# Sums of weight blocks made by adding transfers on GpSimd's queue, and the seven products of a pair in another order

## The reference

```
def _squared_relu_mlp(h, w1, w2):
    return jnp.square(jax.nn.relu(h @ w1)) @ w2

for layer in range(DEPTH_2):
    ...
    x = x + _rms_norm(mix, norm_mix_post[layer])
    hn = _rms_norm(x, norm_ffn_pre[layer])
    x = x + _rms_norm(_squared_relu_mlp(hn, mlp_w1[layer], mlp_w2[layer]), norm_ffn_post[layer])
```

## Time and profile before

| | us |
|---|---|
| median of 3 runs | 1752.04 (1751.86 to 1753.19) |
| the profiled execution | 1751.83 |
| its span | 1750.1 |
| TensorE busy in the span | 1720.5 |
| VectorE busy | 1058.1 |
| ScalarE busy | 869.3 |
| GpSimd busy | 367.2 |

### The profile page before, as it was taken

One profiled execution on the slowest core, in us unless ns is written; L12 is line 12 of the kernel. 1 busy time (PEld: TensorE's weight loads), 2 busy tenths in 40 slices (PEclk: granted clock), 3 DMA queues, 4 the chain that ended last, 5 costly groups with the idle time before them and its releaser, 6 DMA issues.

```text
span 1750.1 us, 21182 instructions
## 1 busy us (share of the span) xinstructions
PE 1720.5 (98%) x8319; PEld 1376.0 (79%) x8319; DVE 1058.1 (60%) x1408; ACT 869.3 (50%) x1410; POOL 367.2 (21%) x197
## 2 busy tenths in 40 slices
PE   7999999999999999999999999999999999999998
PEld 5888777778787767876988888888876798888886
DVE  6611567685976367954467576745457247686855
ACT  4324566557635353254563535336677356354542
POOL 0443322123244233433400000004410330000000
PEclk9999999999999999999999999999999999999999
DMA  8524322221132322311232231322320241414031
GB/s 314 209 92 120 97 61 60 74 73 55 67 121 80 109 73 72 108 49 57 91 131 100 93 128 65 121 73 64 96 66 1 97 145 48 147 47 169 25 130 75
DMA packets 83935, 166.25 MB, mean 95 GB/s; under 512 B 6041, under 2 KB 8222, under 8 KB 83838
## 3 DMA queue, kind: packets, MB, share of 16 engines
q1 hardware_dynamic: 83838, 164.93, 28.3%
HBM read 157.64 MB, written 2.10 MB: 91 GB/s over the span
## 4 chain that ended last, share of the span: by engine, by line
PE 92%; DVE 4%; ACT 2%; issue 1%; POOL 1%; DMA 0%; SPq 0%; DVEq 0%; ACTq 0%; POOLq 0%
PE PDT L779 10%; PE PDT L781 10%; PE PDT L780 10%; PE PDT L768 9%; PE PDT L770 8%; PE PDT L769 8%; PE PM L970 4%; PE PM L965 4%; PE PM L963 4%; PE PM L1153 2%; PE PM L1427 2%; PE PDT L1388 2%; PE PM L1388 2%; PE PM L1120 1%; PE PM L1180 1%
## 5 line engine op out<-in xcount | busy, mean ns | idle before, releaser
L2201 POOL TENSOR_TENSOR wlo<-wraw,whi 128x512 fp32r<-128x512 f32 (+5 forms) x112 | 324.2, 2911 | 933.6 <-ACT whi L1589 758.8
L779 PE MATMUL PDT<-hhi,whi 128*128 128x512 f32 x796 | 312.3, 392 | 0.5 <-POOL wlo L2201 0.5
L781 PE MATMUL PDT<-hhi,wlo 128*128 128x512 f32 x796 | 310.2, 390 | 0.0
L780 PE MATMUL PDT<-hlo,whi 128*128 128x512 f32 x796 | 310.1, 390 | 0.0
L1705 ACT ACTIVATE whi<-wraw 128x2048 fp32r<-128x2048 f32 x78 | 149.5, 1917 | 276.1 <-PE PM L970 120.5
L2876 DVE TENSOR_TENSOR wlo<-wraw,whi 128x2048 fp32r<-128x2048 f32 x78 | 178.7, 2291 | 160.9 <-ACT whi L1705 160.7
L768 PE MATMUL PDT<-whi,hhi 128*128 128x512 f32 (+1 forms) x592 | 233.4, 394 | 1.1 <-DVE hlo L2611 0.6
L770 PE MATMUL PDT<-whi,hlo 128*128 128x512 f32 (+1 forms) x592 | 227.9, 385 | 0.0
L769 PE MATMUL PDT<-wlo,hhi 128*128 128x512 f32 (+1 forms) x592 | 227.8, 385 | 0.0
L1589 ACT ACTIVATE whi<-wraw 128x2048 fp32r<-128x2048 f32 (+3 forms) x71 | 129.3, 1821 | 173.7 <-PE PDT L770 75.8
L779 PEld LDWEIGHTS PDT<-hhi,whi 128*128 128x128 f32 x796 | 149.5, 188 | 31.5 <-issue 1.5
(11 more groups left out here) (409 smaller groups left out, 2873.5 us busy)
## 6 DMA issues: line engine op xcount, KB each, us to landing
wraw<-in_mlp_w SPq DMA_DIRECT2D x64, 1024.0 KB, 5.1
wraw<-in_w_in SPq DMA_DIRECT2D x26, 1024.0 KB, 5.1
wraw<-in_even_w_in SPq DMA_DIRECT2D x16, 1024.0 KB, 5.2
w_ada<-in_w_ada SPq DMA_DIRECT2D x11, 1024.0 KB, 12.9
wraw<-in_w_out SPq DMA_DIRECT2D x8, 1024.0 KB, 4.9
swapped<-qk_sb SPq DMA_DIRECT2D x16, 256.0 KB, 7.2
wraw<-in_even_w_out SPq DMA_DIRECT2D x4, 1024.0 KB, 4.9
wraw<-in_odd_w_o SPq DMA_DIRECT2D x4, 1024.0 KB, 4.9
```

The lines of the kernel that those rows point to most:

```text
L779: mm(bank, sth, hi[:, k0 + k, :], start=start and k == 0, stop=False)
L780: mm(bank, sth, lo[:, k0 + k, :], start=False, stop=False)
L781: last = mm(bank, stl, hi[:, k0 + k, :], start=False, stop=stop and k == 3)
L2201: part = g.tensor_tensor(wlo[base % 2][:, cols], wraw[base % 2][:, cols], fl(whi[base % 2][:, cols]), ALU.subtract)
```

## The change

Four things change, all in the two MLPs except for the last.

1. The sums of blocks of `w2` are no longer made by VectorE. GpSimd issues transfers from HBM that add what they bring onto what stands in the slot (`accum_op=ALU.add`), five per pair, and each waits for the one before it (semaphore `w_added`). Slot e gets B11 by a plain load, then two transfers make it the operand of P6, and a fifth, after P6's split, that of P4. Slot b gets B12 and one transfer, for P7. P1's slot gets one transfer after P1's split, for P5. ScalarE's `raw_hi` waits on `w_added` for these four (`ADDED`, `SUMMED`).
2. The seven products come in the order P1, P2, P6, P5, P7, P3, P4 (before: P1, P5, P6, P2, P7, P3, P4), and VectorE's low parts and additions follow it.
3. SyncE loads five plain blocks per pair instead of four, B11 twice and B22 and B21 for P3 and P2, in another order and into slots by another rule (`pair_loads`).
4. The space for descriptors of software transfers is 2048 bytes instead of 1024, the arena of buffers starts at a multiple of 64 bytes instead of 512, and the small tile `scratch1` lies in the arena.

The core of the diff:

```diff
@@ -67,11 +67,20 @@
 MLP_UNITS = 41
 CHUNKS = [0, 2, 4, 13, 15, 24, 26, 35]
 PAIRED = [6, 17, 28]
-ROLES = [(2, 3, 0, 1), (1, 3, 0, 2), (2, 3, 0, 1)]
-MLP_LOADS = [(0, 0), (1, 1), (2, 2), (3, 3), (4, 0), (5, 1),
-             (6, 2), ("b", 6, 3), (11, 0), (9, 1), (13, 1), (14, 3), (15, 0), (16, 2),
-             (17, 1), ("b", 17, 3), (22, 0), (20, 2), (24, 2), (25, 3), (26, 0), (27, 1),
-             (28, 2), ("b", 28, 3), (33, 0), (31, 1), (35, 1), (36, 3), (37, 0), (38, 2), (39, 3), (40, 2)]
+P1, P2, P6, P5, P7, P3, P4 = range(7)
+
+
+def pair_loads(d, a, e, b, plain):
+
+    return [((d, "e"), e), ((d, P1), a), ((d, P2), plain), ((d, "b"), b), ((d, P3), plain)]
+
+
+MLP_LOADS = [((0, 0), 0), ((1, 0), 1), ((2, 0), 2), ((3, 0), 3), ((4, 0), 0), ((5, 0), 1)]
+MLP_LOADS += pair_loads(6, 3, 2, 1, 0) + [((13, 0), 3), ((14, 0), 1), ((15, 0), 0), ((16, 0), 2)]
+MLP_LOADS += pair_loads(17, 1, 3, 2, 0) + [((24, 0), 1), ((25, 0), 2), ((26, 0), 0), ((27, 0), 3)]
+MLP_LOADS += pair_loads(28, 2, 1, 3, 0) + [((35, 0), 2), ((36, 0), 3), ((37, 0), 0), ((38, 0), 1), ((39, 0), 2),
+                                           ((40, 0), 3)]
+SUMMED = {P6: ("e", 2), P7: ("b", 3), P5: (P1, 4), P4: ("e", 5)}
 
 
 def phase_table():
@@ -113,9 +122,13 @@
 
     for name, (u0, _, _, units) in PH.items():
         if name in ("mlp0", "mlp1"):
-            for *key, slot in MLP_LOADS:
+            for (d, part), slot in MLP_LOADS:
                 slot = (u0 + slot) % 2 if slot < 2 else slot
-                load(u0 + key[0] if len(key) == 1 else (u0 + key[1], "b"), slot)
+                load((u0 + d, part) if isinstance(part, str) else u0 + d + part, slot)
+            for p, d in enumerate(PAIRED):
+                for n, (part, done) in SUMMED.items():
+                    of = table[u0 + d, part] if isinstance(part, str) else table[u0 + d + part]
+                    table[u0 + d + n] = (of[0], 16 * (15 * (name == "mlp1") + 5 * p + done))
         else:
             for u in range(u0, u0 + units):
...
-    A0 = (cursor[0] + 511) // 512 * 512
+    A0 = (cursor[0] + 63) // 64 * 64
...
             for p, d in enumerate(PAIRED):
                 c = 2 * p
                 split(CHUNKS[c + 1])
+                down((u0 + d, "e"), c, 0)
+                split(CHUNKS[c + 1] + 1)
                 down(u0 + d + P1, c, 0)
-                split(CHUNKS[c + 1] + 1)
+                split(CHUNKS[c + 2])
+                down(u0 + d + P2, c + 1, 0)
+                split(CHUNKS[c + 2] + 1)
                 down((u0 + d, "b"), c, 1)
-                split(CHUNKS[c + 2])
+                split(d + P2)
                 down(u0 + d + P3, c + 1, 1)
-                split(CHUNKS[c + 2] + 1)
-                down(u0 + d + P2, c + 1, 0)
+                split(d + P5)
+                up(c + 3, 0)
                 split(d + P7)
-                up(c + 3, 0)
                 up(c + 3, 1)
                 split(d + P3)
                 if p < 2:
...
                 product(P1, 0, True, base)
-                product(P5, 1, True, 0)
+                product(P2, 1, True, 0)
                 product(P6, 0, False, base + 1)
-                product(P2, 1, True, base + 3)
-                product(P7, 0, False, base + 4)
+                product(P5, 1, True, base + 2)
+                product(P7, 0, False, base + 3)
                 product(P3, 1, True, base + 5)
                 product(P4, 0, False, base + 6)
...
-            def raw_hi(o, slot=None, summed=0):
+            def raw_hi(o):
 
                 u = u0 + o
-                if summed:
-                    act.wait_ge(S("w_summed"), 12 * layer + summed)
-                elif u in RAW:
-                    slot, loaded = RAW[u]
-                    act.wait_ge(S(f"w_loaded{slot}"), loaded)
+                slot, loaded = RAW[u]
+                act.wait_ge(S("w_added" if (u0, o) in ADDED else f"w_loaded{slot}"), loaded)
                 act.wait_ge(S("w_used"), u - 1)
...
+
+            def added(key, c, h, count, after=None):
+
+                slot, loaded = RAW[key]
+                if count > 1:
+                    pool.wait_ge(S("w_added"), 16 * (count - 1))
+                pool.wait_ge(S(f"w_loaded{slot}"), loaded)
+                if after is not None:
+                    pool.wait_ge(S("w_split"), u0 + after + 1)
+                g.dma_start(wview(wraw[slot], 4, 512), w2_v[layer][:, 4 * c:4 * c + 4, 512 * h:512 * h + 512],
+                            accum_op=ALU.add).then_inc(S("w_added"), 16)
+
+            for p, d in enumerate(PAIRED):
+                c, n = 2 * p, 15 * layer + 5 * p
+                added((u0 + d, "e"), c, 1, n + 1)
+                added((u0 + d, "e"), c + 1, 1, n + 2)
+                added((u0 + d, "b"), c + 1, 1, n + 3)
+                added(u0 + d + P1, c, 1, n + 4, d + P1)
+                added((u0 + d, "e"), c + 1, 0, n + 5, d + P6)
...
-            def add_raw(to, other, loaded):
-
-                slot, value = RAW[loaded]
-                dve.wait_ge(S(f"w_loaded{slot}"), value)
-                v.tensor_tensor(wraw[to][:, :], wraw[to][:, :], wraw[other][:, :], ALU.add).then_inc(S("w_summed"), 1)
...
             def products(p):
 
-                a, b, c, d = [(u0 + slot) % 2 if slot < 2 else slot for slot in ROLES[p]]
                 o = PAIRED[p]
-                add_raw(a, c, u0 + o + P3)
-                gather(p, P1, 0, 0, 0, ALU.add, -3)
-                add_raw(b, c, u0 + o + P3)
-                raw_lo(o + P6, a)
+                gather(p, P1, 0, 0, 0, ALU.add, -6)
+                raw_lo(o + P6)
+                gather(p, P2, 1, 0, 0, ALU.add, 1)
+                raw_lo(o + P5)
+                gather(p, P6, 0, 0, 1, ALU.subtract, -1)
+                raw_lo(o + P7)
                 gather(p, P5, 1, 1, 1, ALU.subtract, -2)
-                gather(p, P5, 1, 0, 1, ALU.subtract, -1)
-                raw_lo(o + P2)
-                add_raw(a, d, u0 + o + P2)
-                gather(p, P6, 0, 0, 1, ALU.subtract, 3)
-                raw_lo(o + P7, b)
-                gather(p, P2, 1, 0, 0, ALU.add, 1)
+                gather(p, P5, 1, 0, 1, ALU.subtract, 3)
                 raw_lo(o + P3)
-                gather(p, P7, 0, 1, 1, ALU.subtract, 2)
-                raw_lo(o + P4, a)
-                gather(p, P3, 1, 0, 1, ALU.subtract, 4)
+                gather(p, P7, 0, 1, 1, ALU.subtract, 4)
+                raw_lo(o + P4)
+                gather(p, P3, 1, 0, 1, ALU.subtract, 5)
                 raw_lo(o + 7)
                 gather(p, P4, 0, 1, 0, ALU.add, 0)
...
-                a, b = [(u0 + slot) % 2 if slot < 2 else slot for slot in ROLES[p][0:2]]
-                add_raw(a, b, (u0 + PAIRED[p], "b"))
-                raw_lo(PAIRED[p] + P5, a)
+                raw_lo(PAIRED[p] + P2)
                 products(p)
...
-    nc = bacc.Bacc("TRN2", target_bir_lowering=False, num_devices=1, dynamic_dma_scratch_size=1024)
+    nc = bacc.Bacc("TRN2", target_bir_lowering=False, num_devices=1, dynamic_dma_scratch_size=2048)
```

32 lines of the change are left out of this document (10 added, 22 removed).

## The result

| | before | after |
|---|---|---|
| median (20 runs each) | 1752.03 us | 1755.11 us |
| lowest to highest | 1751.81 to 1755.07 | 1753.69 to 1758.00 |
| the profiled execution | 1751.83 | 1754.89 |
| its span | 1750.1 | 1752.7 |

The ratio is 1.0017, with a 95% interval of 1.001 to 1.0024: 3.1 us slower. I had forecast 1752.0 and no change. The range holds the time, the forecast doesn't. Of the 3.1 us, 2.6 are in the span of the profiled executions, and some 0.5 outside it (2.2 us there for 1.7). Of all the executions behind this document, one, in experiment 7, fell into a slower state (2457.7 us at a mean granted clock of 0.66, where the three others of that kernel have 0.99), and it is left out there.

A forecast was written before the change was run, and what follows sets the result against it. TensorE was taken to bound the kernel, its work covering all else; the terms summed as 0 - 0 + 0, leaving the profiled execution at 1751.83 us and the predicted median at 1752.0, range 1749.5 to 1770.

The forecast's parts named there:

- What bounds the kernel: Whole span: TensorE, busy 1720.5 of 1750.1 us, is the bound; time saved on VectorE, ScalarE or GpSimd there shortens nothing.
- rival C: Norms' waits for VectorE, 3.1 us: faster since VectorE loses 54.8 us of work; 1749 if all went; chance 0.04.
- The adding transfers: GpSimd's queue in the MLPs: 30 transfers of 1 MB, all landing before they are wanted; cost 0.
- X: Time of one adding transfer on GpSimd's queue, issue through landing: taken as 7.5 us, range 5.0 to 17.5.
- The limit at the fourth transfer: ScalarE's rounding for P5: X may be 12.5 (first pair) or 13.0 us; above, each pair loses twice the excess.
- Order, loads and bank pairs: MLP pairs: new product order, one more plain load per pair and sums on the bank pairs all in time; cost 0.
- Rival B: GpSimd's descriptor writing, kept back by VectorE in the MLP pairs: 12.8 us slower at X = 8.5, 1765; chance 0.07.
- Addresses: Arena start at a multiple of 64 bytes, small tile moved in, descriptor space doubled: no added instruction, taken as 0.
- rival A: ScalarE's rounding for P5: the chain of adding transfers becomes the bound, 1778 us at X = 15; chance 0.18.
- Outside the span: Time of the profiled execution around its span: taken as unchanged at 1.7 us.

The follow-up runs named there:

- experiment 7: Kernel of experiment 1 with adding transfers made twice: all, 1954.4 us; only the fourth of each pair, 1772.53 us; first, second and fifth, 1846.76 us.
- experiment 1: The changed kernel with its arena at a multiple of 512 bytes again and descriptor space 1536 bytes for 2048: 1753.53 us, ratio 1.0005.
- experiment 2: The kernel before with only its arena moved up by 448 bytes, to the changed kernel's address: 1755.09 us, ratio 1.002.

## Why the prediction was wrong

*What bounds the kernel: right.* TensorE is the bound, and it is in both kernels. 49 us less on VectorE brought nothing, and rival C had no place. The sentence that under 0.2% a measurement can't tell from no change was too careful: 20 executions of each kernel told 0.17% from nothing.

*The adding transfers: right in what they cost, wrong in their own length.* I took X = 7.5 and measured 8.8, 12.0 at most. The limit that I worked out was 12.5, and the one wait of ScalarE, 2.4 us, stayed covered. The choice of the nearest row, 2048 KB because a sum reads two blocks, was better than that of a plain load of 1 MB (5.0). But 7.5 was still 1.3 too low. By the Trainium skill ("DMA: Bandwidth & Descriptors", "Anatomy of one DMA — SWDGE (gpsimd) path"), 2.0 us and the bytes at 436 GB/s, the estimates are 4.4 us for 1 MB and 6.8 for 2 MB, and the measurement is over both.

*The limit at the fourth transfer: right, its price half right.* The fourth transfer made twice gave 11.9 us of waiting for 11.6. The price left out that the clock can fall behind a wait, and that above some 13.7 us per transfer (an estimate: 81.6 less 13.2, over five transfers) the chain closes to a loop, with 5 us per pair for each microsecond of X instead of 2.

*Order, loads and bank pairs: right.* With the address as before, all of these together are at most 0.14% by the interval of experiment 1, and a pair takes 81.60 us there as before.

*Rival B: the changed kernel's trace speaks against it.* A transfer should take longer where VectorE is busier. Here are the windows of the first and the second transfer of the second pair, from issue to landing:

```profile
core 0: us, PE busy (x) PEld busy (x) DVE busy (x) ACT busy (x) POOL busy (x), PEclk, DMA share, GB/s
966.00:978.00 12.00, 12.00 (x54) 9.94 (x53) 2.29 (x1) 3.40 (x4) 1.28 (x1) 1.00 0.82 178
978.40:986.80 8.40, 8.40 (x38) 6.96 (x38) 7.71 (x12) 8.30 (x13) 1.29 (x1) 1.00 1.01 244
```

The slower one, 12.0 us, had VectorE busy for 2.3 us, and the faster one, 8.4 us, for 7.7. The first transfer is the slowest of its pair in five of the six pairs, 11.0 to 12.0 us; why, no run separates. No run took VectorE's work away to measure it by itself. The work in these windows is TENSOR_TENSOR but for two SCALAR_TENSOR_TENSOR of 0.69 us, which the prediction overlooked when it called it all TENSOR_TENSOR.

*"Addresses": here it failed.* The prediction said: "That adds no instruction; I take 0, though no row tells addresses apart." That was the step. It cost 2.4 us of the profiled span and 3.2 by the medians of experiment 2 (1755.09 beside 1751.87): all of the loss but the half microsecond outside the span. In place of 0, each of 1392 matmuls came about 2.3 ns later. I named an unknown, and then neither bounded it from both sides, as I did for X, nor made it a rival. The bound was at hand: the arena holds the stationary operand of 1392 matmuls, and one nanosecond on each is 1.4 us; 2.5 ns are enough to leave the 0.2% that I had called no change. With 72% on "within 0.2%", an unknown that touches the bounding engine in 1392 places was worth far more than the 3%, all of it for a gain, that I gave it. "That adds no instruction" was an argument about the count of matmuls, and the time is count by pace. That the range still holds 1755.1 is luck: its upper part was room for rival A, which didn't come.

*Outside the span: slightly wrong.* I took 1.7 us as it was, and it is 1.8 to 2.4, some 0.5 us of the loss. Its cause is open.

## What to carry to other kernels

A change's side edits (where a buffer starts, how it is rounded) count when they touch an operand of the bounding engine: write down how many instructions read it, and price one nanosecond on each. Keep the operands of matmuls of 512 columns in this format on a multiple of 256 bytes, above all the stationary ones, and look at the mean of one matmul by group and not only at the busy share, which stays at 100% when the pace falls. Where work is moved to a chain of transfers, look for the loop that the chain closes over a period, as well as for the first deadline; above a limit the clock and then the loop can make the price steeper than the excess.
